# A decoder layer on one core: the output product takes the first half of w_out for all four prompt tiles, then the second

## The reference

```python
h = _rmsnorm(x, g_pre_mix) * (1.0 + sc1) + sh1
...  # h @ w_in, HGRN2 branch o_a, differential attention branch o_b
merged = jax.nn.sigmoid(gate_a) * (o_a @ w_proj_a) + jax.nn.sigmoid(gate_b) * (o_b @ w_proj_b)
x = x + gt1 * _rmsnorm(merged @ w_out, g_post_mix)
h2 = _rmsnorm(x, g_pre_ffn) * (1.0 + sc2) + sh2
x = x + gt2 * _rmsnorm(_moe(h2, w_router, b_router, w_gate_up, b_gate_up, w_down, b_down), g_post_ffn)
```

## Time and profile before

| what | us |
|---|---|
| median of 3 runs (lowest, highest) | 1266.66 (1265.62, 1268.01) |
| span of the profiled execution | 1266.6 |
| TensorE busy with matmuls | 1087.7 (86%) |
| VectorE busy | 597.7 (47%) |
| ScalarE busy | 224.9 (18%) |
| GpSimd busy | 60.0 (5%) |

### The profile page before, as it was taken

The page is one execution under the profiler, slowest core; times in us unless marked ns, Lnnn a source line. Parts: engine busy times, 40 slices in busy tenths (PEclk is TensorE's granted clock), DMA queues, the critical chain, the costliest instruction groups (busy, mean ns, idle before and its releaser), DMA issues.

```text
span 1266.6 us, 23750 instructions
## 1 busy us (share of the span) xinstructions
PE 1087.7 (86%) x9790; PEld 462.8 (37%) x9790; DVE 597.7 (47%) x1126; ACT 224.9 (18%) x371; POOL 60.0 (5%) x106
## 2 busy tenths in 40 slices
PE   6999999999888796995788978999866996667996
PEld 3776777784422131331222322333211331112332
DVE  3537744344654352553353643666432552333654
ACT  3002410132311110111011111211111111101112
POOL 0312020310200000000000000000000000000000
PEclk9999999999889898998897999999987998889999
DMA  9979894696899999999999999999999999999996
GB/s 344 306 246 355 316 331 144 212 352 267 321 416 427 428 429 428 428 428 428 428 428 428 426 428 410 394 422 428 428 427 429 427 428 427 428 427 429 428 428 246
DMA packets 67282, 486.16 MB, mean 384 GB/s; under 512 B 6013, under 2 KB 28882, under 8 KB 40426
## 3 DMA queue, kind: packets, MB, share of 16 engines
q1 hardware_dynamic: 59584, 462.11, 88.2%
q0 software_dynamic: 6496, 19.48, 4.7%
q10 hardware_dynamic: 1130, 3.50, 0.8%
HBM read 479.31 MB, written 5.77 MB: 383 GB/s over the span
## 4 chain that ended last, share of the span: by engine, by line
DMA 45%; PE 26%; DVE 1%; issue 0%; ACT 0%; DVEq 0%; ACTq 0%
DMA big<-in_w_down 28%; PE PB L1147 13%; DMA big<-in_w_gate_up 12%; PE PB L1174 7%; DMA hTG<-in_w_down 5%; PE PB L1108 2%; PE PB L1116 2%; PE PB L1132 1%; PE PB L1123 1%; PE PB L1140 0%; PE PB L1093 0%; DVE big L1476 0%; DVE cst L1473 0%; DVE big L1473 0%; ACT L1419 0%
## 5 line engine op out<-in xcount | busy, mean ns | idle before, releaser
L1147 PE MATMUL PB<-big,cst 128*32 128x512 f32 x2768 | 354.3, 655 | 109.5 <-DMA big<-in_w_gate_up 109.5
L2057 DVE TENSOR_TENSOR tok<-PB,cst 32x512 f32<-32x512 f32 x188 | 129.1, 687 | 257.9 <-ACT cst L1418 255.9
L1147 PEld LDWEIGHTS PB<-big,cst 128*32 128x32 f32 x2768 | 88.7, 115 | 346.3 <-issue 182.6
L1174 PE MATMUL PB<-big,cst 128*32 128x512 f32 x1408 | 165.0, 597 | 20.9 <-DMA big<-in_w_down 20.9
L719 PE MATMUL PB<-hTG,big 128*128 128x264 f32 x576 | 138.1, 394 | 1.5 <-DVE hTG L1470 1.5
L2034 DVE TENSOR_SCALAR mod<-PB 64x512 f32<-64x512 f32 x48 | 33.3, 693 | 208.0 <-PE PB L1147 207.9
L719 PEld LDWEIGHTS PB<-hTG,big 128*128 128x128 f32 x576 | 107.8, 192 | 28.9 <-issue 11.8
L1413 ACT ACTIVATE mod<-PB 64x512 f32<-64x512 f32 x48 | 28.4, 592 | 420.4 <-PE PB L1147 420.4
L1108 PE MATMUL PB<-wide,att 128*32 128x256 f32 x1176 | 80.3, 406 | 5.5 <-DVE att L2029 5.5
L1174 PEld LDWEIGHTS PB<-big,cst 128*32 128x32 f32 x1408 | 38.9, 109 | 104.4 <-issue 64.9
L1108 PEld LDWEIGHTS PB<-wide,att 128*32 128x32 f32 x1176 | 39.7, 115 | 61.0 <-issue 36.7
(11 more groups left out here) (346 smaller groups left out, 909.2 us busy)
## 6 DMA issues: line engine op xcount, KB each, us to landing
big<-in_w_gate_up SPq DMA_DIRECT2D x115, 2048.0 KB, 30.9
big<-in_w_down SPq DMA_DIRECT2D x57, 2048.0 KB, 23.7
hTG<-in_w_gate_up SPq DMA_DIRECT2D x13, 2048.0 KB, 38.6
big<-in_w_mod SPq DMA_DIRECT2D x24, 1024.0 KB, 7.6
big<-in_w_in SPq DMA_DIRECT2D x22, 1024.0 KB, 9.0
hTG<-in_w_down SPq DMA_DIRECT2D x6, 2048.0 KB, 24.1
wide<-in_cache_k POOLq DMA_DIRECT2D x16, 256.0 KB, 5.9
big<-in_w_out SPq DMA_DIRECT2D x4, 1024.0 KB, 10.1
```

The lines of the kernel that those rows point to most:

```text
L1147: mm = pe.matmul(GU[32 * j:32 * j + 32, :], mo["xT"][:, (2 * u + r) * M:(2 * u + r + 1) * M], groups(w[:, r * 2 * D:(r + 1) * 2 * D])[:, j ...
L1174: mm = pe.matmul(DN[32 * j:32 * j + 32, :], mo["actT"][:, (4 * u + r) * M:(4 * u + r + 1) * M], w[:, r * D + half * 512:r * D + (half + 1) ...
L2057: mm = dve.tensor_tensor(mo["y"][rows, :], DN[rows, :], mo["y_part"][other, :], ALU.add)
```

## The change

The order of TensorE's instructions is changed, and one place in the rotation of the small PSUM banks. The first half of w_out (s = 0 to 3) is used for all four prompt tiles before the second half is used for any of them. The samples' two products stand between the first halves of chunk 0 and of chunk 1. The transposes of the samples' x1 come behind the first halves, then chunk 0's second halves, the samples' logits, and chunk 1's second halves. The transposes of chunk 0's x1, which stood ahead of the samples' logits, now come behind the last tile, followed by chunk 0's logits. `AUX_ORDER` takes rt2 ahead of xa0 and xa1 accordingly. `wo_half_used` is signalled by the same instruction as before. The orders of the other engines are not changed.

```diff
-AUX_ORDER += "ys0 ys1 xs xa0 xa1 rt2 rt0 xb0 xb1 rt1 pos".split()
+AUX_ORDER += "ys0 ys1 xs rt2 xa0 xa1 rt0 xb0 xb1 rt1 pos".split()
...
-            out_rows(0, 0).then_inc(S("yo_full"), 1)
+            out_rows(0, 0, 0, 4)
+            out_rows(0, 1, 0, 4)
             pe.wait_ge(S("yt_ready"), 2)
             for i in range(2):
                 full(pe.matmul(begin(f"ys{i}")[0:NS, :], C("selt"), ytile[:, i * 512:(i + 1) * 512],
                                start=True, stop=True))
-            out_rows(0, 1).then_inc(S("yo_full"), 1)
-            x1_T(2, 0, "xs")
             out_rows(1, 0, 0, 4)
             out_rows(1, 1, 0, 4).then_inc(S("wo_half_used"), 1)
-            x1_T(0, 2, "xa0", "xa1")
+            x1_T(2, 0, "xs")
+            out_rows(0, 0, 4, KC).then_inc(S("yo_full"), 1)
+            out_rows(0, 1, 4, KC).then_inc(S("yo_full"), 1)
             logits(2)
             for i in range(2):
                 out_rows(1, i, 4, KC).then_inc(S("yo_full"), 1)
+            x1_T(0, 2, "xa0", "xa1")
             logits(0)
             x1_T(1, 4, "xb0", "xb1")
```

## The result

| | before | after |
|---|---|---|
| median of 9 runs (lowest, highest), us | 1266.99 (1265.62, 1274.41) | 1278.25 (1274.35, 1285.64) |
| ratio to before, 95% interval | | 1.0075 [1.0051, 1.0099] |
| span of the profiled execution, us | 1266.6 | 1272.7 |

The change makes the kernel slower, by 0.75%. The ratio times the median of before gives 1276.5 us, interval 1273.5 to 1279.5; the forecast was 1274.7, range 1270.5 to 1278.0. The plain median of the nine runs lies 0.25 us above that range.

A forecast was written before the change was run, and what follows sets the result against it. The prediction took the expert-weight stream to bound the kernel, its restart set by the last prompt chunk's routing. Wait 3.2, copies 2.6 and clock 2.2 sum to 8.0 us: 1266.66 + 8.0 = 1274.7 us, range 1270.5 to 1278.0.

The forecast's parts named there:

- The wait ahead of the samples' logits: TensorE idles 4.0 us before logits(2) until VectorE's scaling behind residual(0); last tile 3.2 us later.
- The copies ahead of the squares: ScalarE copies chunk 0's transposes before squaring chunk 1's tiles; sum of squares 3.5 us behind last tile, +2.6 us.
- The clock: TensorE's clock halves after the 4.0 us idle stretch, slowing the products behind it: +2.2 us, bounds 0 to 3.8.
- the row at 755: Earlier trace: after 2.97 us idle at 752 to 755, 16 products took 3.56 us instead of 1.92; loss 1.6 us.
- the one at 357: Earlier trace: after idle 351.65 to 357.19, clock low until about 362.6; loss 2.7 us.
- The sum: 3.2 + 2.6 + 2.2 = 8.0 us later restart, at 354.6 instead of 346.57; time 1274.7 us.
- the restart: Eleventh expert-weight load, issued at 346.57 once the first expert's first unit is used; its delay delays the end equally.
- Nothing behind the restart changes: From the restart to the end the kernel runs as before, so the restart's 8.0 us delay carries to the end.
- The earlier load is worth nothing: Load 4 goes at 310.65 instead of 318.33, 7.7 us earlier, but buys nothing while the restart stays.
- The rival in which the end follows the bytes: Early load 4 fills 4.9 us of idle DMA time ahead of the restart; end at 1261.8 us; chance 0.04.
- the second rival: Clock stays low longer or falls again in chunk 1's transposes and logits: +10 to +12 us, 1277 to 1279; chance 0.13.
- the bank of rt2: Other condition of ScalarE's copies: VectorE gives this bank back near 327, so it adds no wait.

The follow-up runs named there:

- halves_only: Kernel before, with chunk 0's two tiles done in halves and nothing moved past chunk 1; ratio 1.0002 to before.
- xs_scale_early: Changed kernel, with VectorE scaling the samples' transposes before chunk 0's gains; ratio 1.0011 to before.
- logits_between: Changed kernel, with the samples' logits between the second halves of chunk 1's two tiles on TensorE; ratio 1.0024 to before.
- transposes_late: Kernel before, with only chunk 0's transposes moved behind the last tile and the bank order that goes with it; ratio 1.0003 to before.
- filled_idle: Changed kernel, with four 128x512 products into an unused bank in TensorE's wait ahead of the samples' logits; ratio 1.0047 to before.
- after_again: The changed kernel run once more as it is, for a second execution; ratio 1.0068 to before.
- before_filled_two: Kernel before, with one product of constants ahead of chunk 1's transposes and two ahead of the last mask; ratio 1.0015 to before.
- load4_late: Changed kernel, with load 4 waiting for the last tile as load 5 does; ratio 1.0062 to before.
- both_orders: Changed kernel, with the samples' transposes scaled early on VectorE and chunk 0's copies behind chunk 1's root on ScalarE; ratio 1.0033 to before.
- after: The changed kernel itself against the kernel before; median 1278.25 us, ratio 1.0075.
- copies_behind_root: Changed kernel, with ScalarE's copies of chunk 0's transposes moved behind chunk 1's squares and root; ratio 1.0056 to before.
- before_filled: Kernel before, with three products of constants in TensorE's wait for the last chunk's mask; ratio 0.9993 to before.

## Why the prediction was right

Its steps, with what the changed kernel's trace has for each:
- *The wait ahead of the samples' logits*: 4.0 us forecast, 4.12 found, ended by the instruction named. `logits(2)` starts 27.79 us behind the product's start, forecast 27.7. halves_only, xs_scale_early and logits_between show that it is the order and nothing else in the edit.
- *The copies ahead of the squares*: sum of squares 3.5 us behind the last tile, found 3.50. transposes_late has this term alone: +1.7 us net of the transposes that leave the place ahead of the tile.
- *The clock*: forecast +2.2 with bounds of 0 and 3.8, found 8.83 - 7.13 = 1.70. The mechanism was right and the size 0.5 us too large: I had averaged the row at 755 with the one at 357, and the one at 755 (1.64) was the nearer. filled_idle shows it by taking it away. The reading of the earlier trace rows behind it was wrong: behind 330 the kernel before has nineteen idle times of 2.9 us or more that began at full clock, not four, and the clock was low at the end of each or fell within 1.2 us of it; of eleven of about 2.6 us, five went the same way. So the fall was surer than the forecast made it.
- *The sum*: 8.0 us forecast for the restart; 7.51 found (51.93 to 59.44), 7.04 in the second execution. From the sum of squares to the restart it is 18.76 us, before 18.87. That these are so near is partly luck, as told below.
- *Nothing behind the restart changes*: 919.15 and 920.8 us to the end, before 920.03. Held within 1 us. Without before_filled_two (923.2), all executions take 918.6 to 921.4.
- *The earlier load is worth nothing*: 0.1 to 1.2 us by load4_late. Held, but with less room than I gave it. I wrote that the DMA engines have no backlog at 346. True, but they had been busy up to 345, hardly more than 1.5 us ahead of the restart; before_filled_two shows that a restart 2.4 us earlier already runs into the last of the ten loads. The rival in which the end follows the bytes was 1 to 2 us away.

The luck is in the second rival. Its condition came true: the clock fell at 336.25, in chunk 1's transposes, `logits(1)` took 3.46 us instead of 1.94, and it ended 2.7 us later behind the sum of squares than before (343.70 - 334.79 against 333.89 - 327.70). The forecast has no term for that, and none was needed. Of the 2.7 us, 1.0 was covered, since before VectorE came to these logits 1.0 us behind their end. Another 1.0 came back from VectorE itself. Its 128x128 operation ahead of the mask, before and after the change, with GpSimd's row ahead of it:

```profile
336.15 1.25 POOL L590 TENSOR_TENSOR wide<-wide,gpost 128x512 f32<-128x512 f32 x1
336.25 1.31 DVE L1473 TENSOR_TENSOR cst<-cst,small 128x128 f32<-128x128 f32 x1
...
343.24 1.25 POOL L590 TENSOR_TENSOR wide<-wide,gpost 128x512 f32<-128x512 f32 x1
344.90 0.29 DVE L1475 TENSOR_TENSOR cst<-cst,small 128x128 f32<-128x128 f32 x1
```

Before, it ran beside GpSimd's operation and took 1.31 us; after, it came behind it and took 0.29. By the time of the gather 0.5 us was left, and the clock, back at 350.0 ahead of the first unit's products (before at 345.5, 1.8 us into them), made up for the rest. Load 9, which waits for `logits(1)`, moved by 9.8 us and not by 6 to 8.

What the prediction didn't see is the third limit. It said that ScalarE's other condition, the bank of rt2, was met near 327, which is true in the changed kernel because the copies come at 331.8. But it took VectorE's work on chunk 0 to be covered, and that cover holds only as long as the other two losses stand: without them VectorE costs 2 us more (both_orders, 54.23 for 52.2). This changed nothing in the forecast of the whole and made the forecast of the repair wrong.

The measured ratio, +8.6 to +9.5 us in two sets of runs, stands above the 6.6 to 7.8 us that the two profiled executions have between product and end; the intervals, 5 to 12.5 us, hold both. The profiled executions are the fastest of their sets of nine and eight (1274.35 and 1274.77), so they may show less than the typical loss. Whether other executions lose more behind the restart, I can't say from two profiles. The forecast's sentence that nothing lies around the span is wrong too: every run with both numbers on record takes 1.6 to 1.8 us more than its span. It falls out of the difference.

## What to carry to other kernels

When an instruction is moved past others on one engine, look up each wait that it carries and write down when the awaited thing is made under the new order; here one small product with an old wait held up 7 us of large ones. Move the matching instructions on the other engines too, or their old order becomes the new limit, and after each repair ask which engine is late next. Freeing a slot for a load earlier pays only where the stream of loads, rather than the work that frees the slots behind it, ends last; here the two were 1 to 2 us apart, so making one of them earlier alone buys next to nothing.

## What the runs showed of the hardware

- An idle time of 4.12 us between dense float32 products was followed by TensorE's fall from 2.4 to 1.2 GHz at 322.5, and the clock came back at 326.0; the eight products behind took 8.83 us, not 7.13. The fall came in all four executions with this wait (after, after_again, copies_behind_root, load4_late). With four products in that idle time (filled_idle) the clock held.
- In thirteen of the fourteen traces the clock fell between 331.25 and 340.75, among or just behind the transposes and the 32-column logits that follow the last tile, and in nine `logits(1)` took 3.46 us instead of 1.87 to 1.94. Where it falls differs between executions of nearly the same work. With one 128x512 product ahead of chunk 1's transposes (before_filled_two) the fall came 39.8 us behind the product's start, in before_filled 36.3, in halves_only 36.3 and in the kernel before 40.6; so nothing shows that the added product holds it off.
- VectorE's 128x128 operation ahead of chunk 1's mask took 1.31 to 1.32 us in the five executions in which it ran beside GpSimd's 128x512 operation (before, after_again, copies_behind_root, both_orders, before_filled_two), and 0.29 us in the nine in which it started behind it. Those nine are the ones with the slow `logits(1)`, which is one reason why these 1.5 us hardly show in the distances.
- The start of the output product varied from 293.3 to 301.5 us between executions of the same instructions. The difference is there by 50 us, and it is TensorE's speed at the start of the span. The rows show records of L719: up to 31 us in filled_idle (output product at 301.54), the same in the changed kernel (294.11), and in the kernel before where its clock was at 0.50 from 25 to 28:

```profile
L719 PE MATMUL PB<-hTG,big x7: 647/647/777, 28.2 to 31.0; 128*128 128x264 f32 x7
L719 PE MATMUL PB<-hTG,big x17: 386/386/386, 27.6 to 31.2; 128*128 128x264 f32 x17
L719 PE MATMUL PB<-hTG,big x9: 478/647/647, 24.5 to 27.9; 128*128 128x264 f32 x9
```

  The three numbers with slashes are the shortest, median and longest in ns. At 28 to 31 us the median is 644 to 648 ns in the six executions whose output product starts at 298.6 or later, and 386 in the eight in which it starts at 296.9 or earlier. The clock column shows 1.00 in filled_idle there, but 647 ns is what these records take at 0.50 in the kernel before; the trace's first entry of the clock is its rise at 33.3 us in filled_idle and at 15.4 in the changed kernel, so I read the 1.00 ahead of it as no reading. Why the clock comes up at 14 us in one execution and at 33 in another stays open.
